# Expert weights of a one-core decoder layer fetched in twelve 1 MB pieces, each contiguous in memory, instead of six 2 MB pieces

## The reference

```python
def expert_block(args):                       # tok: up to a block of tokens, e: the expert
    tok, wr, e = args
    hb = xpad[tok] @ mlp1_w[e] + mlp1_b[e]    # 1024 -> 2048
    yb = clamped_swiglu(hb) @ mlp2_w[e] + mlp2_b[e]   # 1024 -> 1024
    return yb * wr[:, None]
```

## Time and profile before

| | |
|---|---|
| device time, median of 3 runs (range) | 1376.84 us (1374.29 to 1377.96) |
| device time of the profiled execution | 1376.84 us |
| its span, from first to last instruction | 1375.1 us |
| mean granted TensorE clock | 0.977 |
| TensorE matmul busy | 1307.8 us, 95% |
| VectorE, ScalarE busy | 353.8 us (26%), 192.1 us (14%) |
| chain that ended last | PE 61%, DMA 32%, DVE 4% |
| moved by DMA | 442.40 MB |

### The profile page before, as it was taken

How to read it: one execution, slowest core, us unless ns; L and a number is a source line. 1 busy time by engine, 2 the same in 40 slices (tenths; PEclk the granted TensorE clock), 3 DMA queues, 4 the chain that set the end, 5 groups by cost and what they waited for, 6 DMA issues and landing times.

```text
span 1375.1 us, 20536 instructions
## 1 busy us (share of the span) xinstructions
PE 1307.8 (95%) x8342; PEld 707.9 (51%) x8342; DVE 353.8 (26%) x843; ACT 192.1 (14%) x457; POOL 43.3 (3%) x98
## 2 busy tenths in 40 slices
PE   7999889879898999999999999999999999999998
PEld 6898777758786334333443344433334333334333
DVE  3364642341224412112121122211212211212212
ACT  2242234411231000000000000000000000000000
POOL 7100001100000000000000000000000000000000
PEclk9999988999997999999999999999999999999999
DMA  7354211119631889999999999999999999999996
GB/s 236 123 120 129 70 55 32 33 32 372 239 131 39 367 344 422 428 430 428 429 428 428 429 429 428 428 429 428 429 429 427 429 428 428 429 428 428 429 429 269
DMA packets 75833, 442.40 MB, mean 322 GB/s; under 512 B 18720, under 2 KB 49550, under 8 KB 50958
## 3 DMA queue, kind: packets, MB, share of 16 engines
q1 hardware_dynamic: 75630, 441.26, 78.5%
q0 software_dynamic: 160, 0.52, 0.1%
HBM read 440.72 MB, written 1.05 MB: 321 GB/s over the span
## 4 chain that ended last, share of the span: by engine, by line
PE 61%; DMA 32%; DVE 4%; ACT 1%; issue 1%; POOL 0%; SPq 0%; DVEq 0%; ACTq 0%
DMA sb_ring<-in_mlp_w 32%; PE ps L906 20%; PE ps L356 9%; PE ps L958 8%; PE ps L684 6%; PE ps L879 4%; PE ps L888 2%; PE ps L555 2%; PE ps L917 1%; PE ps L717 1%; PE ps L407 1%; PE ps L425 1%; DVE sb_qx L994 1%; ACT sb_ring L1478 1%; PE ps L945 0%
## 5 line engine op out<-in xcount | busy, mean ns | idle before, releaser
L906 PE MATMUL ps<-sb_ring,sb_hnT 128*64 128x512 f32 x2016 | 454.1, 598 | 10.8 <-DMA sb_ring<-in_mlp_w 10.8
L906 PEld LDWEIGHTS ps<-sb_ring,sb_hnT 128*64 128x64 f32 x2016 | 136.2, 137 | 322.8 <-issue 269.2
L958 PE MATMUL ps<-sb_ring,sb_hnT 128*64 128x512 f32 x1024 | 226.8, 595 | 0.0
L958 PEld LDWEIGHTS ps<-sb_ring,sb_hnT 128*64 128x64 f32 x1024 | 70.6, 137 | 133.4 <-issue 133.4
L1443 DVE TENSOR_SCALAR sb_wsl<-ps 128x256 f32<-128x256 f32 x64 | 26.8, 419 | 414.8 <-PE ps L906 414.8
L879 PE MATMUL ps<-sb_wsl,sb_h 128*128 128x64 f32 x1056 | 125.0, 278 | 1.2 <-DVE sb_wsl L1329 1.2
L879 PEld LDWEIGHTS ps<-sb_wsl,sb_h 128*128 128x128 f32 x1056 | 123.8, 196 | 1.3 <-DVE sb_wsl L1329 1.3
L1478 ACT ACTIVATE sb_wsl<-sb_wsl 128x256 f32<-128x256 f32 x64 | 26.6, 416 | 555.5 <-DVE sb_wsl L1443 555.5
L356 PE MATMUL ps<-sb_hnT,sb_wsl 128*128 128x256 f32 x448 | 98.8, 380 | 1.8 <-DVE sb_hnT L1008 0.9
L1478 ACT ACTIVATE sb_hnT<-ps 128x256 f32<-128x256 f32 (+1 forms) x112 | 51.0, 456 | 295.7 <-PE ps L958 212.6
L356 PEld LDWEIGHTS ps<-sb_hnT,sb_wsl 128*128 128x128 f32 x448 | 84.8, 190 | 14.2 <-DVE sb_hnT L1008 1.2
(11 more groups left out here) (344 smaller groups left out, 944.6 us busy)
## 6 DMA issues: line engine op xcount, KB each, us to landing
sb_ring<-in_mlp_w SPq DMA_DIRECT2D x190, 2048.0 KB, 22.5
sb_wsl<-in_w_in SPq DMA_DIRECT2D x10, 1024.0 KB, 5.8
sb_wsl<-in_xk_w SPq DMA_DIRECT2D x4, 1024.0 KB, 5.1
sb_wsl<-in_xv_w SPq DMA_DIRECT2D x4, 1024.0 KB, 5.1
sb_wsl<-in_xq_w SPq DMA_DIRECT2D x4, 1024.0 KB, 10.1
sb_wsl<-in_xo_w SPq DMA_DIRECT2D x4, 1024.0 KB, 5.1
sb_wsl<-in_w_in SPq DMA_DIRECT2D x8, 256.0 KB, 4.3
sb_wsl<-in_w_out SPq DMA_DIRECT2D x8, 256.0 KB, 4.1
```

What stands on the lines that cost most here:

```text
L906: mm = pe.matmul(psum[64 * half:64 * half + 64, 4 + n, :], xgT[:, k, :], w[:, at + 512 * half:at + 512 * half + 512], start=False, stop=k ...
L958: mm = pe.matmul(psum[64 * o2:64 * o2 + 64, 7, :], actT[:, 2 * n + m, 64 * q:64 * q + 64], ring[:, at + 512 * o2:at + 512 * o2 + 512], sta ...
```

## The change

The six parts of 4096 columns become twelve of 2048 columns, 1 MB each (`pieces`), and the weights are laid out in HBM so that each part of each expert is one contiguous block of 128 x 2048 numbers: 8 KB for each partition, one partition's after the other's. The four parts that are fetched ahead for item 1 keep size and target, but are contiguous now too. TensorE waits and releases per 1 MB; the thresholds of VectorE and ScalarE are the same points of the work in the new count. The products, their operands in SBUF and their order are unchanged, and so are all other transfers. The early fetch of item 0 takes two parts where it took one.

```diff
-PIECE = 4096
-PIECES = 24576 // PIECE
-W1_PIECES = 8192 // PIECE
+        pieces = [view(ring, 2048 * c, 2048) for c in range(12)]
...
             def hidden(i, n, first, second):
-                for k in range(KD):
-                    at = 8192 * n + 1024 * k
-                    c = at // PIECE
...
+                for kp in range(4):
+                    c = 4 * n + kp
                     if second and n == 0:
-                        if at % 2048 == 0:
-                            pe.wait_ge(sem(f"ahead_in_{k // 2}"), 16)
+                        pe.wait_ge(sem(f"ahead_in_{c}"), 16)
                     else:
...
+                        pe.wait_ge(sem(f"piece_in_{c}"), (i + 1) * 16 if first or n else i * 16)
+                    w = ahead[c] if second and n == 0 else pieces[c]
+                    for k2 in range(2):
+                        for half in range(2):
+                            at = 1024 * k2 + 512 * half
+                            mm = pe.matmul(psum[64 * half:64 * half + 64, 4 + n, :], xgT[:, 2 * kp + k2, :],
+                                           w[:, at:at + 512], start=False, stop=kp == 3 and k2 == 1)
+                    mm.then_inc(sem("piece_used"), 1)
...
-                at = slice(PIECE * c, PIECE * (c + 1))
-                sp.dma_start(ring[:, at], a["mlp_w"][bass.ds(e, 1), :, at].rearrange("e p f -> p (e f)")) \
+                sp.dma_start(pieces[c], a["mlp_w"][bass.ds(e, 1), c].rearrange("e p f -> p (e f)")) \
                   .then_inc(sem(f"piece_in_{c}"), 16)
...
-                if j >= J_OUT + 2 and left and (j - J_OUT) % 1 == 0:
-                    piece(0, left.pop(0))
+                if j >= J_OUT + 2:
+                    for c in left[:2]:
+                        piece(0, c)
+                    left = left[2:]
...
                 for c in which:
-                    sp.wait_ge(sem("piece_used"), i * PIECES + (c + 1 - PIECES))
+                    sp.wait_ge(sem("piece_used"), i * 12 + (c - 11))
                     piece(e, c)
...
-            for c in range(W1_PIECES):
+            for c in range(4):
                 sp.wait_ge(sem("piece_used"), c + 1)
                 piece(2, c)
-            item(1, 1, range(W1_PIECES, PIECES))
-            item(2, 2, range(W1_PIECES, PIECES))
+            item(1, 1, range(4, 12))
+            item(2, 2, range(4, 12))
...
-    w = np.empty((NE, P, 24576), np.float32)
+    w = np.empty((NE, 12, P, 2048), np.float32)
```

More of the change, by code:

```diff
@@ L226, in build @@
         reve = sb("reve", NE)
-        aheads = [view(buf, 0, 2048) for buf in (ox, mixT[:, :, :].rearrange("p a b -> p (a b)"), vx, qx)]
+        pieces = [view(ring, 2048 * c, 2048) for c in range(12)]
+        ahead = [view(buf, 0, 2048) for buf in (ox, mixT[:, :, :].rearrange("p a b -> p (a b)"), vx, qx)]
         def vec(name, i=0, n=1):
@@ L892, in hidden @@
             def hidden(i, n, first, second):
-                for k in range(KD):
-                    at = 8192 * n + 1024 * k
-                    c = at // PIECE
+                for kp in range(4):
+                    c = 4 * n + kp
                     if second and n == 0:
-                        if at % 2048 == 0:
-                            pe.wait_ge(sem(f"ahead_in_{k // 2}"), 16)
-                        w, at = aheads[k // 2], at % 2048
-                    else:
[L902 to L909, removed]
+                        pe.wait_ge(sem(f"ahead_in_{c}"), 16)
+                    else:
+                        pe.wait_ge(sem(f"piece_in_{c}"), (i + 1) * 16 if first or n else i * 16)
[6 more added lines that the diff above has]
+                    mm.then_inc(sem("piece_used"), 1)
             def item(i, first=False, second=False):
@@ L952, in item @@
                     for q in range(2):
+                        c = 8 + 2 * n + q
+                        pe.wait_ge(sem(f"piece_in_{c}"), (i + 1) * 16)
                         for m in range(2):
-                            at = 16384 + 4096 * n + 2048 * q + 1024 * m
-                            if at % PIECE == 0:
-                                pe.wait_ge(sem(f"piece_in_{at // PIECE}"), (i + 1) * 16)
                             for o2 in range(2):
+                                at = 1024 * m + 512 * o2
                                 mm = pe.matmul(psum[64 * o2:64 * o2 + 64, 7, :],
[L959 to L963, removed]
+                                               actT[:, 2 * n + m, 64 * q:64 * q + 64], pieces[c][:, at:at + 512],
+                                               start=c == 8 and m == 0, stop=c == 11 and m == 1)
+                        mm.then_inc(sem("piece_used"), 1)
             pe.wait_ge(sem("selected"), 1)
@@ L1438, in item @@
                 for n in range(2):
-                    dve.wait_ge(sem("piece_used"), i * PIECES + W1_PIECES * (n + 1))
+                    dve.wait_ge(sem("piece_used"), i * 12 + 4 + 4 * n)
                     if n == 1:
@@ L1762, in item @@
                       ACT.Copy).then_inc(sem("act_out"), 1)
-                act.wait_ge(sem("piece_used"), i * PIECES + PIECES)
+                act.wait_ge(sem("piece_used"), i * 12 + 12)
                 f(yb, psum[:, 7, :], ACT.Copy).then_inc(sem("y_out"), 1)
@@ L1971, in piece_ahead @@
                     sp.wait_ge(sem("tile_ready"), tiles["xout", 3][1] + 1)
-                sp.dma_start(aheads[c], a["mlp_w"][1, :, 2048 * c:2048 * (c + 1)]).then_inc(sem(f"ahead_in_{c}"), 16)
-            left = list(range(PIECES))
+                sp.dma_start(ahead[c], a["mlp_w"][1, c]).then_inc(sem(f"ahead_in_{c}"), 16)
+            left = list(range(12))
             for j in range(WSLOTS, len(JOBS)):
@@ L1978, in _, with item @@
                     sp.wait_ge(sem("rwkv_out"), 2)
-                if j >= J_OUT + 2 and left and (j - J_OUT) % 1 == 0:
-                    piece(0, left.pop(0))
+                if j >= J_OUT + 2:
+                    for c in left[:2]:
+                        piece(0, c)
+                    left = left[2:]
             for c in range(4):
                 piece_ahead(c)
-            def item(i, e, which=range(PIECES)):
+            def item(i, e, which=range(12)):
                 for c in which:
-                    sp.wait_ge(sem("piece_used"), i * PIECES + (c + 1 - PIECES))
+                    sp.wait_ge(sem("piece_used"), i * 12 + (c - 11))
                     piece(e, c)
-            for c in range(W1_PIECES):
+            for c in range(4):
                 sp.wait_ge(sem("piece_used"), c + 1)
                 piece(2, c)
-            item(1, 1, range(W1_PIECES, PIECES))
-            item(2, 2, range(W1_PIECES, PIECES))
+            item(1, 1, range(4, 12))
+            item(2, 2, range(4, 12))
             with sp.Fori(3, NE - 1) as i:
@@ L2020, in laid_out @@
 def laid_out(inputs):
-    w = np.empty((NE, P, 24576), np.float32)
-    w1 = inputs["mlp1_w"][0].reshape(NE, KD, P, 2, 2, 256, 2)
-    w[:, :, 0:16384].reshape(NE, P, 2, KD, 2, 2, 256)[...] = w1.transpose(0, 2, 3, 1, 4, 6, 5)
+    w = np.empty((NE, 12, P, 2048), np.float32)
+    w1 = inputs["mlp1_w"][0].reshape(NE, 4, 2, P, 2, 2, 256, 2)
+    w[:, 0:8].reshape(NE, 2, 4, P, 2, 2, 2, 256)[...] = w1.transpose(0, 4, 1, 3, 2, 5, 7, 6)
     w2 = inputs["mlp2_w"][0].reshape(NE, 2, 2, 2, P, D)
-    w[:, :, 16384:].reshape(NE, P, 2, 2, 2, D)[...] = w2.transpose(0, 4, 1, 2, 3, 5)
+    w[:, 8:12].reshape(NE, 2, 2, P, 2, D)[...] = w2.transpose(0, 1, 2, 4, 3, 5)
     b1 = inputs["mlp1_b"][0].reshape(NE, 2, 2, 256, 2).transpose(1, 2, 0, 4, 3).reshape(P, 512)
```

## The result

The changed kernel takes 1383.33 us (median of 5 runs, 1383.02 to 1384.19) against 1375.98 us in the same comparison: a ratio of 1.0057, with a 95% interval of 1.0043 to 1.0072. Timed again later, beside other runs of the kernel before, it took 1383.52 us, a ratio of 1.0062 (1.0045 to 1.0079). It is slower by 7.3 us in both comparisons (by the intervals 5.9 to 9.9 and 6.2 to 10.9); the forecast was 1385.5 us, +8.7.

The account below looks back on a forecast made before the run. The DMA stream was taken to bound the kernel through the whole expert stage. From 1376.84 us, +13.1 for shorter runs, -2.4 for early refills and -2.0 at the tail gave 1385.5 us; 8 in 10 range 1373.5 to 1391.

Parts of the forecast that it names:

- The reading of the bound: Expert stage: the DMA stream, 29.38 us per item against TensorE's 28.32, sets the end even where the chain names TensorE.
- both regimes: Expert-stage chain: only TensorE up to about 850 us, every 28.32 us; from 856.67 alternating with ring transfers, 29.38 us per item.
- The rate: Steady stream of items 3 to 31: 8 KB runs lower 428 GB/s to 422, period 29.84 us, +13.1 us.
- the one 1 KB window: Projection weights at 20 to 25 us: 348 GB/s, 3.013 us per MB, giving 9.4 ns per run.
- The direct window: Item 1's 8 KB-run transfers at 405 to 409 us: 424 GB/s, 2.473 us per MB, 25 ns more than now.
- The early refills: Last dry spot, W2 of item 1: first 1 MB refill issued 1.85 us after its start; gain 2.4 us (1.7 to 3.1).
- The tail: Last wait, in H1 of item 31: half of 3.65 us remains after it instead of all; -2.0 us together.
- At nothing: TensorE's added waits, clock at 1.00, SP's 12 issues per item of some 0.35 us, item 0's early fetch: 0 us.
- Sum: Whole kernel: +13.1 - 2.4 - 2.0 = +8.7 us, from 1376.84 to 1385.5 us.
- the rate stays: Steady stream: cost hangs on bytes, not runs, so only the gains remain, -4.4, 1372.4 us; chance 0.18 including a rising rate.
- the rate falls further: Steady stream: transfer-end gaps or neighbouring blocks hinder the engines; at 416 GB/s +25 - 4.4, 1397.6 us; chance 0.12.

## Why the prediction was right

- **The reading of the bound** held: the stream is busy throughout both regimes, and the price of a slower stream was paid in full, also for the items in which the chain names only TensorE.
- **The rate** was the term that decided. Expected 422 GB/s, 29.84 us per item and +13.1 us; measured 422, 29.82 and, from 29.38, 29 x 0.445 = +12.9. The 9.4 ns for each run, drawn from the one 1 KB window of the earlier trace rows, fits at the two other steps: from 16 to 8 KB (2.485 - 2.448) / 4 = 9.3 ns, from 32 to 16 KB (2.448 - 2.429) / 2 = 9.5 ns. The direct window alone would have said 25 ns per MB, a third too little. That one window of 5 us gave a price good to 2% is partly luck: the 8 GB/s by which such windows scatter in the prediction's own account would move it by about 1.2 ns, or 12%.
- **The early refills** were over-sized: 2.4 us expected (1.7 to 3.1), 1.3 measured. Reckoned back as in the prediction, the last part of item 2 lands at 1359.92 + 4 x 2.485 - 29 x 29.82 = 505.1, 15.9 us after C, before 509.8 - 492.6 = 17.2. The issue came 1.97 us after C (1.85 expected); the start-up, reckoned the same way, took 4.0 us, just beyond the slow end of 3.7. The timeline of the changed kernel:

```profile
489.17 4.08 PE L953 MATMUL ps<-sb_ring,sb_hnT 128*64 128x512 f32 x18
491.14 2.04 SPq L1953 DMA_DIRECT2D sb_ring<-in_mlp_w  x2
```

The mechanism was only half right. The prediction held that the dry spot in W2 of item 1 resets the stream, so that earlier gaps don't count, and that a share above 0.90 from 490 to 500 us would show the gain; the share was 0.90. But the stream was not empty there: when that part was issued, the one before it hadn't landed, in either kernel (before: issue at 496.29, landing at 496.98; after: 491.14 and 492.39). The ten microseconds up to C and the ten after it, before and after the change:

```profile
482.60:492.60 10.00, 10.00 (x67) 5.88 (x63) 2.06 (x6) 0.69 (x2) 0.00 (x0) 1.00 0.68 269
492.60:502.60 10.00, 10.00 (x51) 3.17 (x52) 1.69 (x6) 0.98 (x2) 0.00 (x0) 1.00 0.91 359
479.17:489.17 10.00, 10.00 (x67) 5.88 (x63) 2.06 (x6) 0.69 (x2) 0.00 (x0) 1.00 0.81 323
489.17:499.17 10.00, 10.00 (x51) 3.17 (x52) 1.69 (x6) 0.98 (x2) 0.00 (x0) 1.00 0.91 365
```

Ahead of C the finer parts move 54 GB/s more, 0.54 MB or 1.3 us of the stream; behind it nearly the same. In the second profiles it is 269 and 324, then 359 and 362. So most of the gain comes from the refills of item 2 in H1 of item 1, the earlier gap that the prediction left out, and little from the one that it counted.

- **The tail**: -2.0 expected; L to end fell by 1.7, and the last MB of H1 lands 0.1 further ahead of the stream's end, -1.8 together.
- **At nothing**: the clock stayed at 1.00 and the first landing in the chain came at 823 us, near the 830 of the forecast. A to C is 183.1 us in one profile of the changed kernel, as before, and 184.7 in the other; the kernel with 2 MB blocks shows 184.8 too, so that is no cost of the change. SP's issues were taken at 0.35 us each; in the steady stream they took 1.51 us on the average (193 issues, 291 us), 18 us per item and not 4.2. That this cost nothing was foreseen for the right reason: behind each issue stands only the next refill. Where something else stands behind, as in the run with 4 MB parts, a held issue holds that too.
- **Sum**: +12.9 - 1.3 - 1.8 = +9.8 by the reckoned terms, 9.7 by the stages. +8.7 was forecast; the difference of 1.1 is the early refills. The measured +7.3 is nearer to the forecast than to this sum; that part is scatter ahead of A and no merit of the forecast.
- **The rivals**: "the rate stays" fell to the windows, "the rate falls further" as well. The experiment with two 8 KB runs in a 2 MB transfer shows that the cost is the run's; the end of a transfer costs too little to be seen beside it. The Trainium skill's page DMA: Bandwidth & Descriptors, section "Bandwidth", gives about 10.5 ns per packet for a 4 KB transfer; the 9.3 to 9.5 ns per run measured here are near it. The advice of the same page in the Trainium skill to lay tiles out contiguously (section "Latency and other measured facts") is given for row pitches from 512 KB up; at 96 KB it bought nothing here.

## What to carry to other kernels

When a stream never pauses, its rate is the kernel's time, also while the chain of waits still names another engine; compare the periods of both before splitting a transfer. Cutting a transfer along the partition row pays for its finer waits with more runs: here 9.4 ns per run and engine, 0.44 us per 12 MB, 12.9 us in all, against 3.1 us of gains that arise only at the two ends. Cut finely only where the stream stops, lengthen the runs in the middle, and let several fine items go ahead of the last wait. Fine parts at the start alone brought 0.4 us or less here, since the next item lost again what they gained; why it did is open. Count every dry spot by what the queue still holds, not by the share alone; and when two profiles differ, first compare the stretch ahead of the first changed instruction.

## What the runs showed of the hardware

Time per MB of a steady stream into 128 partitions, by length of the contiguous run: 3.013 us at 1 KB (one window of 5 us), 2.485 at 8 KB, 2.448 at 16 KB, 2.429 at 32 KB. Whether the runs lay 96 KB apart or end to end made no difference to the rate (422 and 422 at 8 KB, 428 and 429 at 16 KB). A run of 32 KB was moved whole. When the stream had nearly run dry, the first of four 1 MB transfers landed 4.78 us after its issue, 2.3 us more than its data take, as a lone one does; the second landed 4.13 us after the first and the others 2.49 apart, so 1.6 us more were lost there, 4.0 in all (4.02 us between the first two in the second profile). What the 1.6 us are was not tried. An issue of a 1 MB transfer took SP 0.33 us with fewer than nine before it not yet landed, and mostly 1.9 us (up to 3.5) with ten or more, both profiles alike; why is not shown.
